# Modulation sums moved wholly to VectorE, with late fetches and a folding reduction

## The chip, the cores and the metric

One core of a Trainium2 chip runs the whole program. The metric is device time in microseconds from the first to the last instruction of one execution; a kernel's figure is the median of its runs.

## The reference

Two blocks run one after the other on 256 tokens of width 1024. Block 1 has two layers (three mixing branches, a gated feed-forward with 2816 hidden columns, a small gated embedding). Block 2 has two layers whose norms and residuals are modulated by vectors that depend on a conditioning vector `c` (for the latents) and `c_ctx` (for the context):

```python
s_lat = jax.nn.silu(c)
s_ctx = jax.nn.silu(c_ctx)[None, :]
for i in range(DEPTH):
    sh1, sc1, g1, sh2, sc2, g2 = jnp.split(s_lat @ ada_w[i] + ada_b[i], 6, axis=-1)
    a_l = modulate(rms_norm(h_lat, norm_g[i, 0]), sh1, sc1)
    if ctx_in:
        csh1, csc1, cg1, csh2, csc2, cg2 = jnp.split(s_ctx @ ada_w[i] + ada_b[i], 6, axis=-1)
```

`ada_w` is 2 x 1024 x 6144, 50 MB in fp32. The change concerns the product of these two vectors with `ada_w` alone. The product depends on nothing that block 1 computes, so it can be made during block 1.

## The kernel before

All weights come through one stream of 555 chunks of 128 x 1024 fp32 (512 KB each), in the order `ORDER`, into a ring of `RING` = 5 buffers `raw`. SP issues the fetch into a buffer when the chunk that is in it has been used up, strictly in order. A weight chunk ("split") is copied by ScalarE (ACT) into `whi` (line 1399, rounded to fp32r) and its remainder is put by GpSimd (POOL) into `wlo` (line 929, in four pieces for the chunks of each layer's first half, in one piece after that). ACT may write a `whi` buffer once TensorE (PE) has opened the chunk four ahead of it in the order; so PE, ACT and POOL walk along the stream together. A product of 128 x 256 takes per 128 rows of weights three matmuls (lines 980, 983, 984: high by high, high by low of the activations, low of the weights by high); a feed-forward tile `hg` or `hu` has 8 x 3 of them and uses one chunk, a down tile `dn` 11 x 3 and 1.375 chunks. Results go to four PSUM banks in rotation, counted by the semaphores `gemm_done` and `tiles_out`: PE may start tile n + 4 once VectorE (DVE) has moved tile n out. Each engine runs its own instruction list in order; the lists are written by loops over `TILES`.

A modulation chunk ("ada", later "mod") also sits in the stream and holds a `raw` buffer until it has been used. Before the change they are used in two ways:

- Block 2's layer 0 (the first 48 chunks): 12 tiles `("ada", n)` per layer of block 1, each two chunks and 8 fp32 matmuls with `silu_c` as stationary (function `modulation`, line 994; the trace shows each fp32 matmul as two). DVE adds each to `rows` (lines 1927, 1930). After four of them a tile `("turn", n)` turns the rows into columns (line 1002), and DVE adds the bias (line 1937). Four stand in the head of the layer (before `u` 1, `gl` 0, `("ss", "q")` and `rotk`), four among the third branch's gates, four in the feed-forward.
- Block 2's layer 1 (the last 48 chunks): in the first MLP of block 2, DVE multiplies each chunk's rows by the factor of their partition and adds them up in `mod_sums` in SBUF (`modulation_sum`, lines 1905 and 1907), and a tile `("sum", half)` for each of 12 half-parts adds the 128 partitions with matmuls of one column (line 1252): 16 of them, as the trace counts, for the 4 half-parts of both samples, 8 for the other 8.

The feed-forward of block 1 is evicted by DVE like this: a tile `hg` by one operation (line 2202); a tile `hu` by four (lines 2205, 2207, 2210, 1859), with ACT's tanh and copy between them; a tile `dn` by one (line 2199). In the head, ACT's square roots for the two small norms (line 1503) stand behind the `whi` copies that `keep_ahead` and `split_for` place there.

Of the kernel before, what the change touches and what calls it, by code (L numbers as in the profile page):

```python
# [61 lines left out]
for _name, _w in (("mix_g", 8), ("gate_b", 24), ("conv_w", 16), ("conv_b", 4), ("ba", 4), ("bx", 4), ("lam", 4),  # L62
# [8 lines left out]
            "wo": 8, "hg": 8, "hu": 8, "dn": 11, "pg": 8, "pp": 2, "ada": 0, "turn": 0}  # L71
# [10 lines left out]
ADA_TILES = DEPTH * 6 * D // 256  # L82
LAYER_ADA = 12
PLACES = 4


def with_modulation(tiles, places, first, flush=()):

    out, n, turned = [], first, first // PLACES
    for t in tiles:  # L90
        for _ in range(places.get(t, 0)):
            if n // PLACES > turned:
                out.append(("turn", turned))
# [25 lines left out]
MID_TILES, _n = with_modulation(MID_TILES, {("g", 2, 0): 1, ("g", 2, 2): 1, ("g", 2, 4): 1, ("g", 2, 6): 1}, _n,  # L119
                                flush=(("y", 2, 7),))  # L120
TAIL_TILES, _n = with_modulation(TAIL_TILES, {("hg", 0, 3): 1, ("hg", 0, 6): 1, ("hg", 0, 9): 1, ("dn", 0, 3): 1}, _n,
                                 flush=(("dn", 0, 6),))
assert _n == LAYER_ADA
FF_TILES = TAIL_TILES[TAIL_TILES.index(("hg", 0, 0)):TAIL_TILES.index(("dn", 1, 0))]
PLE_TILES = TAIL_TILES[TAIL_TILES.index(("pg", 0)):]
TILES = HEAD_TILES + MLA_FILL + FOX_FILL + MID_TILES + TAIL_TILES
# [32 lines left out]
ADA_CHUNKS = 2  # L159
assert PLACES * ADA_CHUNKS == KT  # L160


# [3 lines left out]
def chunk_plan(tiles, spans):  # L166

    order, at, adas, late, needed = [("split", n) for n in range(LEAD)], {}, 0, [], 0
    runs = {"ada": ADA_CHUNKS, "mod": 1}
    splits = LEAD  # L170
    for t in tiles:
        if t[1][0] in runs:
            run = [("ada", adas + i) for i in range(runs[t[1][0]])]
            adas += len(run)
# [12 lines left out]
def chunk_reach(tiles, spans, order, at):  # L187

    reach, needed, adas, read = {}, 0, 0, 0
    for t in tiles:  # L190
        first, to = spans.get(t, (0, 0))
# [4 lines left out]
        adas += {"ada": ADA_CHUNKS, "mod": 1}.get(t[1][0], 0)  # L196
        last = at[t] if needed == read else order.index(("split", needed - 1))
        r = min(last + AHEAD, len(order) - 1)
        while r + 1 < len(order):
            kind, n = order[r + 1]  # L200
            freed_by, m = order[r + 1 - RING] if r + 1 >= RING else ("split", 0)
            if kind == "split" and (n >= needed + SLOTS_AHEAD or (freed_by == "ada" and m >= adas)):
                break
            r += 1
        reach[t] = r
# [52 lines left out]
SUM_CHUNKS = 4  # L258
SUM_BEHIND = 2


def with_sums(tiles, places):

    out, n, due = [], 0, []
    for i, t in enumerate(tiles):
        if due and due[0][1] <= i:
            out.append(("sum", due.pop(0)[0]))
        for _ in range(places.get(t, 0)):
            out.append(("mod", n))
            n += 1  # L270
            if n % SUM_CHUNKS == 0:
                due.append((n // SUM_CHUNKS - 1, i + SUM_BEHIND))
        out.append(t)
    assert not due
    return out, n
# [2489 lines left out]
```

## Time and profile before

| what | value |
|---|---|
| median of 3 runs | 1834.68 us (1832.49 to 1835.5) |
| the profiled execution | 1833.74 us |
| its span | 1831.9 us |
| PE busy | 1738.3 us, 95% |
| POOL busy | 1172.0 us, 64% |
| ACT, DVE busy | 893.1 us and 891.2 us, 49% each |
| bytes read | 295.89 MB |

The profiled execution lies 0.94 us below the median, and 1.84 us above its span. Block 1's first layer runs from 0 to about 533 us, its second to about 1050 us, block 2 takes the rest. The feed-forward of the two layers lies at about 308 to 501 us and 824 to 1017 us.

### The profile page before, as it was taken

To read this page: it belongs to the slowest core of one execution; us is meant where nothing else is said; L and a number is where in the kernel's file an instruction comes from. 1 tells how busy PE (TensorE), PEld (TensorE's weight loads), DVE (VectorE), ACT (ScalarE), POOL (GpSimd) and SP (SyncE) were. 2 spreads that over 40 slices of the span, in tenths; PEclk is the share of its full clock that TensorE was granted. 3 is DMA by queue.
4 is the path that set the end of the run, shared out by engine and by line. 5 is a ranking of instruction groups with operands and counts; after the bars stand their busy time and mean duration, and the time that the engine had idled before them with its cause. 6 is when DMAs were issued, how large, how long until landed. Compare 5 with 4: busy or idle time off the path is not lost.

```text
span 1831.9 us, 32203 instructions
## 1 busy us (share of the span) xinstructions
PE 1738.3 (95%) x12690; PEld 1601.1 (87%) x12690; DVE 891.2 (49%) x2019; ACT 893.1 (49%) x1468; POOL 1172.0 (64%) x768
## 2 busy tenths in 40 slices
PE   6899999999999899999999969999999979889997
PEld 6788899999999788999999968888888778689997
DVE  6577445313365674353233666854444565642223
ACT  6545546444666455465445864232323353564443
POOL 6887678788878776677788623444444443058884
PEclk9999999999999899999999989999999999999999
DMA  6543465665555433666655503354453422035552
GB/s 238 192 144 127 133 236 190 226 212 184 176 188 185 154 128 129 235 200 214 219 185 175 199 26 127 140 194 163 171 183 139 172 93 81 24 116 186 182 184 81
DMA packets 83414, 299.02 MB, mean 163 GB/s; under 512 B 9152, under 2 KB 11456, under 8 KB 83008
## 3 DMA queue, kind: packets, MB, share of 16 engines
q1 hardware_dynamic: 81648, 294.02, 47.3%
q10 hardware_dynamic: 1616, 2.95, 0.5%
q8 instruction: 100, 1.64, 0.4%
q14 instruction: 50, 0.41, 0.1%
HBM read 295.89 MB, written 1.05 MB: 162 GB/s over the span
## 4 chain that ended last, share of the span: by engine, by line
PE 84%; DVE 7%; ACT 3%; issue 2%; POOL 2%; DVEq 1%; DMA 1%; ACTq 0%; SPq 0%
PE bank L980 25%; PE bank L984 24%; PE bank L983 24%; POOL wlo L929 2%; PE bank L994 1%; PE bank L1146 1%; PE bank L1160 1%; PE bank L1252 1%; PE bank L1176 1%; ACT whi L1399 1%; PE bank L1223 1%; DVE acts L2103 1%; PE bank L1226 1%; PE bank L1227 1%; PE bank L1149 1%
## 5 line engine op out<-in xcount | busy, mean ns | idle before, releaser
L929 POOL TENSOR_TENSOR wlo<-raw,whi 128x256 fp32r<-128x256 f32 (+1 forms) x756 | 1166.3, 1567 | 638.9 <-ACT whi L1399 638.3
L980 PE MATMUL bank<-split_acts,whi 128*128 128x256 f32 (+1 forms) x3492 | 1058.6, 303 | 26.7 <-DVE split_acts L1859 16.0
L983 PE MATMUL bank<-split_acts,whi 128*128 128x256 f32 (+1 forms) x3492 | 1046.1, 300 | 0.0
L984 PE MATMUL bank<-split_acts,wlo 128*128 128x256 f32 (+1 forms) x3492 | 1046.0, 300 | 0.0
L1399 ACT ACTIVATE whi<-raw 128x1024 fp32r<-128x1024 f32 x459 | 483.6, 1056 | 550.4 <-DMA raw<-in_stream 302.8
L980 PEld LDWEIGHTS bank<-split_acts,whi 128*128 128x128 f32 x3492 | 669.4, 192 | 68.3 <-issue 24.0
L983 PEld LDWEIGHTS bank<-split_acts,whi 128*128 128x128 f32 x3492 | 670.3, 192 | 20.6
L984 PEld LDWEIGHTS bank<-split_acts,wlo 128*128 128x128 f32 x3492 | 669.8, 192 | 21.0
L1859 DVE TENSOR_TENSOR split_acts<-bank,split_acts 128x256 fp32r<-128x256 f32 (+1 forms) x214 | 98.7, 461 | 50.2 <-ACT split_acts L1543 20.9
L2525 DVE SCALAR_TENSOR_TENSOR acts<-bank,acts 128x256 f32<-128x256 f32 x104 | 47.4, 481 | 149.5 <-PE bank L984 149.0
L1907 DVE SCALAR_TENSOR_TENSOR acts<-raw,acts 128x512 f32<-128x512 f32 x112 | 111.9, 1019 | 8.1 <-issue 2.5
L2539 DVE TENSOR_SCALAR acts<-bank 128x512 f32<-128x512 f32 (+1 forms) x64 | 35.6, 558 | 150.0 <-PE bank L984 141.5
L2205 DVE TENSOR_TENSOR bank<-bank,acts 128x256 f32<-128x256 f32 x44 | 19.0, 432 | 102.2 <-PE bank L984 102.2
L1726 ACT ACTIVATE bank<-acts 128x512 f32<-128x512 f32 (+1 forms) x64 | 31.3, 489 | 53.9 <-DVE acts L2539 53.9
L1509 ACT ACTIVATE acts<-acts 128x128 f32<-128x128 f32 (+1 forms) x64 | 28.6, 448 | 50.6 <-DVE acts L2112 50.6
L2196 DVE TENSOR_TENSOR acts<-bank,acts 128x256 f32<-128x256 f32 x32 | 13.6, 425 | 67.8 <-PE bank L984 67.8
L2166 DVE TENSOR_TENSOR acts<-bank,acts 128x256 f32<-128x256 f32 x48 | 20.4, 425 | 49.2 <-PE bank L984 47.3
L1445 ACT ACTIVATE bank<-acts 128x256 f32<-128x256 f32 x56 | 31.7, 566 | 19.6 <-DVE acts L2498 16.5
L1534 ACT ACTIVATE acts<-acts 128x256 f32<-128x256 f32 x48 | 24.2, 505 | 32.2 <-DVE acts L2166 32.2
L1543 ACT ACTIVATE split_acts<-bank 128x256 fp32r<-128x256 f32 x44 | 16.9, 384 | 46.0 <-DVE bank L2210 45.7
L2202 DVE TENSOR_TENSOR bank<-bank,acts 128x256 f32<-128x256 f32 x44 | 19.0, 433 | 36.0 <-PE bank L984 35.5
L1223 PE MATMUL bank<-split_acts,whi 128*128 128x256 f32 (+1 forms) x48 | 18.8, 393 | 18.5 <-DVE split_acts L1859 18.5
(277 smaller groups left out, 1610.5 us busy)
## 6 DMA issues: line engine op xcount, KB each, us to landing
raw<-in_stream SPq DMA_DIRECT2D x555, 512.0 KB, 3.6
acts<-in_x SPq DMA_DIRECT2D x1, 1024.0 KB, 6.1
acts<-in_ctx ACTq DMA_DIRECT2D x1, 1024.0 KB, 7.3
acts<-in_const ACTq DMA_DIRECT2D x1, 1024.0 KB, 5.2
out<-acts SPq DMA_DIRECT2D x8, 128.0 KB, 2.1
acts<-in_const SPq DMA_DIRECT2D x1, 711.0 KB, 8.2
acts<-in_p ACTq DMA_DIRECT2D x2, 256.0 KB, 3.9
acts<-in_const ACTq DMA_DIRECT2D x1, 320.0 KB, 3.0
```

The source lines that it names most:

```text
L929: last = nc.gpsimd.tensor_tensor(wlo[slot][:, cols], raw[source][:, cols], whi[slot][:, cols].bitcast(F32), ALU.subtract)
L980: first = nc.tensor.matmul(out_ap, w_hi, hi_act(k), start=(k == 0), stop=False)
L983: nc.tensor.matmul(out_ap, w_hi, lo_act(k), start=False, stop=False)
L984: last = nc.tensor.matmul(out_ap, w_lo, hi_act(k), start=False, stop=(k == k_tiles - 1))
L1223: one = nc.tensor.matmul(o, w_hi[:, cols], hi, start=(k == 0), stop=False)
L1399: sc.activation(whi[n % RING][:, :], raw[source % RING][:, :], ACT.Copy).then_inc(hi_ready, 1)
L1445: last = sc.activation(dst(t, s), side(tmp, t % 2, s), ACT.Identity, scale=gain_col(l, i, t, s), bias=mod_col(l, SH1 if i == 0 else SH2, t ...
L1726: sc.activation(hid_home[j % 3][:, a], tile(tmp, j % 2, 512)[:, a], ACT.Square)
L1859: return v.tensor_tensor(lo, value, hi.bitcast(F32), ALU.subtract)
L1907: last = v.scalar_tensor_tensor(out=total, in0=w, scalar=factor, in1=total, op0=ALU.mult, op1=ALU.add)
L2525: last = v.scalar_tensor_tensor(out=side(h, n, s), in0=src, scalar=col(s), in1=side(h, n, s), op0=ALU.mult, op1=ALU.add)
L2539: v.tensor_scalar(tile(tmp, j % 2, 512)[:, a], b[:, 0:w], 0.0, None, ALU.max)\
```

## The change

- All 96 modulation chunks are summed on DVE by `modulation_sum`. The 48 for block 2's layer 0 are used in block 1's feed-forward: 24 per layer, one ahead of the eviction of each of `hg` (0, 1 to 9), `dn` (0, 1 to 6) and `hg` (1, 0 to 8). Each has both samples, so four operations of 128 x 512 per chunk. The 48 others stay in block 2's first MLP, at places that shift by a few tiles.
- The partial sums lie in PSUM banks 6 and 7 in block 1, and in `v2` (SBUF) and bank 4 in block 2. `c_square` has two buffers instead of four for it.
- When the four chunks of a half are in, DVE reduces each sum of 128 x 512 to 128 x 16 with a `tensor_reduce` that transposes (line 1878). One tile `("sum",)` per stage (two in block 1, one in block 2) then adds what is left with four matmuls of 48 or 64 columns against a stack of four identities, `fold` (line 976).
- `fetch_tiles` puts a modulation chunk into the stream as if it were needed four tiles later than it is.
- The ada and turn tiles are gone, and `opening_gains` moves to behind `hu` (1, 9) of the second layer.

The core of the diff:

```diff
--- before.py
+++ after.py
@@
+SUM_CHUNKS = 4
+SUM_BEHIND = 2
+def with_sums(tiles, places):
+
+    out, n, last = [], 0, max(tiles.index(t) for t in places)
+    for i, t in enumerate(tiles):
+        if i == last + SUM_BEHIND:
+            out.append(("sum",))
+        for _ in range(places.get(t, 0)):
+            out.append(("mod", n))
+            n += 1
+        out.append(t)
+    return out, n
+FETCH_BEHIND = 4
+def fetch_tiles(tiles):
+
+    out, late, i = [], [], 0
     for t in tiles:
+        if t[0] == "mod":
+            late.append((t, i + FETCH_BEHIND))
+            continue
+        while late and late[0][1] <= i:
+            out.append(late.pop(0)[0])
         out.append(t)
+        i += 1
+    return out + [t for t, _ in late]
...
-HEAD_TILES, _n = with_modulation(HEAD_TILES, {("u", 1): 1, ("gl", 0): 1, ("ss", "q"): 1, ("rotk", 0): 1},
-                                 0, flush=(("kn", 2),))
...
+FFN_PLACES = {**{("hg", 0, j): 1 for j in range(1, 10)}, **{("dn", 0, n): 1 for n in range(1, 7)},
+              **{("hg", 1, j): 1 for j in range(9)}}
...
 MLP_PLACES = [((w, 0, q, j), 1) for q in range(QUARTERS)
-              for w, js in (("w1", range(2, 7) if q == 0 else range(1, 6)),
-                            ("w2", range(8 if q < 2 else 7 if q == 2 else 5))) for j in js]
+              for w, js in (("w1", range(5, 7) if q == 0 else range(1, 7)),
+                            ("w2", range(8 if q < QUARTERS - 1 else 4))) for j in js]
...
-        mod_sums = [[v2[:, (2 * i + s) * 512:(2 * i + s + 1) * 512] for s in range(2)] for i in range(2)]
+        folded = v2[:, 512:768]
...
-        c_square = [bank[4], bank[5], bank[6], bank[7]]
+        c_square = [bank[4], bank[5]]
+        mod_parts = [[bank[6][:, :], bank[7][:, :]]] * DEPTH + [[v2[:, 0:512], bank[4][:, :]]]
...
+            def sum_quadrants(b, stage):
+
+                pe.wait_ge(mod_summed, stage + 1)
+                n = len(SUM_SLOTS[stage])
+                parts = folded[:, 0:16 * n].rearrange("p (m q) -> p m q", q=4)
+                for q in range(4):
+                    nc.tensor.matmul(b[32 * q:32 * q + 32, 0:4 * n], C("fold"), parts[:, :, q], start=True, stop=True)
+                return pe.drain()
...
                 for k in (2 * pair, 2 * pair + 1):
                     v.drain()
                     for s in sides:
-                        w, total = raw[c % RING][:, k % 2 * 512:(k % 2 + 1) * 512], mod_sums[half % 2][s]
+                        w = raw[c % RING][:, k % 2 * 512:(k % 2 + 1) * 512]
                         factor = silu_c[:, 2 * k + s:2 * k + s + 1]
                         if k == 0:
-                            last = v.tensor_scalar(total, w, factor, None, ALU.mult)
+                            last = v.tensor_scalar(parts[s], w, factor, None, ALU.mult)
                         else:
-                            last = v.scalar_tensor_tensor(out=total, in0=w, scalar=factor, in1=total, op0=ALU.mult,
-                                                          op1=ALU.add)
+                            last = v.scalar_tensor_tensor(out=parts[s], in0=w, scalar=factor, in1=parts[s],
+                                                          op0=ALU.mult, op1=ALU.add)
                 last.then_inc(mod_used, 1)
                 if pair == SUM_CHUNKS - 1:
-                    v.drain().then_inc(mod_summed, 1)
...
+                    v.drain()
+                    for s in sides:
+                        i = SUM_SLOTS[stage].index((half, s))
+                        last = v.tensor_reduce(folded[:, 16 * i:16 * i + 16],
+                                               parts[s].rearrange("p (b j) -> p b j", j=32), axis=AXX, op=ALU.add,
+                                               apply_transpose=True)
+                    if half == STAGE_SUMS[stage][-1]:
+                        last.then_inc(mod_summed, 1)
```

The rows that follow are the instruction lists, in order of the program, without times. On PE, in the third branch of layer 0 of block 1, around the tile `("ada", 4)`; before:

```order
L983 MATMUL bank<-split_acts,whi 128x256
L984 MATMUL bank<-split_acts,wlo 128x256
L994 MATMUL bank<-raw,acts 32x256 x8
L980 MATMUL bank<-split_acts,whi 128x256
L983 MATMUL bank<-split_acts,whi 128x256
```

The eight matmuls read the raw chunk; this row is gone at all 24 places. On PE in the feed-forward of layer 0, between `hu` (1, 8) and `hg` (1, 9); now:

```order
L966 MATMUL bank<-split_acts,whi 128x256
L967 MATMUL bank<-split_acts,wlo 128x256
L976 MATMUL bank<-acts 32x48 x4
L963 MATMUL bank<-split_acts,whi 128x256
L966 MATMUL bank<-split_acts,whi 128x256
```

The row with L976 is new; before, the products of the two tiles followed each other directly.

On DVE in the same feed-forward, from the last step of `hu` (0, 0) through `hu` (0, 1) to the chunk ahead of `hg` (0, 2); now (L2164 evicts `hg`, L2167 to L1822 evict `hu`):

```order
L1822 TENSOR_TENSOR split_acts<-bank,split_acts 128x256
L1869 TENSOR_SCALAR bank<-raw,acts 128x512 x2
L1871 SCALAR_TENSOR_TENSOR bank<-raw,acts,bank 128x512 x2
L2164 TENSOR_TENSOR bank<-bank,acts 128x256
L2167 TENSOR_TENSOR bank<-bank,acts 128x256
L2169 SCALAR_TENSOR_TENSOR acts<-acts,bank 128x256
L2172 SCALAR_TENSOR_TENSOR bank<-acts,bank 128x256
L1822 TENSOR_TENSOR split_acts<-bank,split_acts 128x256
L1871 SCALAR_TENSOR_TENSOR bank<-raw,acts,bank 128x512 x4
L2164 TENSOR_TENSOR bank<-bank,acts 128x256
```

The rows L1869 and L1871 are new; each stands ahead of an eviction that PE waits for in the end.

On ACT in the head of a layer of block 1, from the wide square root of the first branch (L1592, now L1555) to the two small ones (L1503, now L1466); before:

```order
L1592 ACTIVATE acts<-acts 128x1024
L1399 ACTIVATE whi<-raw 128x1024 x2
L1503 ACTIVATE acts<-acts 128x256 x2
L1399 ACTIVATE whi<-raw 128x1024 x6
```

and now:

```order
L1555 ACTIVATE acts<-acts 128x1024
L1362 ACTIVATE whi<-raw 128x1024 x4
L1466 ACTIVATE acts<-acts 128x256 x2
L1362 ACTIVATE whi<-raw 128x1024 x4
```

Two more chunks are copied ahead of the small roots, and there are no modulation chunks between the chunks any more.

## Rows read from the trace of the kernel before

**Rows 1.** The page: busy us (share of the span) and instructions of each engine.

```profile
PE 1738.3 (95%) x12690; PEld 1601.1 (87%) x12690; DVE 891.2 (49%) x2019; ACT 893.1 (49%) x1468; POOL 1172.0 (64%) x768
```

**Rows 2.** Busy time by stretch: us, PE, PEld, DVE, ACT, POOL, PE clock, DMA share, GB/s.

```profile
414.00:506.00 92.00, 92.00 (x767) 91.95 (x766) 32.40 (x77) 52.08 (x78) 74.94 (x32) 1.00 0.56 181
```

**Rows 3.** Timeline of PE around an ada tile of the feed-forward: start, duration.

```profile
384.00 0.28 PE L984 MATMUL bank<-split_acts,wlo 128*128 128x256 f32 x1
384.20 1.07 PE L994 MATMUL bank<-raw,acts 128*32 128x256 f32 x16
385.41 0.38 PE L980 MATMUL bank<-split_acts,whi 128*128 128x256 f32 x1
```

**Rows 4.** Timeline of PE around a turn tile (397) and a sum tile (1138).

```profile
397.26 0.28 PE L984 MATMUL bank<-split_acts,wlo 128*128 128x256 f32 x1
...
397.74 0.36 PE L980 MATMUL bank<-split_acts,whi 128*128 128x256 f32 x1
...
1138.40 0.39 PE L983 MATMUL bank<-split_acts,whi 128*128 128x512 f32 x1
1138.63 0.39 PE L984 MATMUL bank<-split_acts,wlo 128*128 128x512 f32 x1
...
1140.56 0.49 PE L980 MATMUL bank<-split_acts,whi 128*128 128x512 f32 x1
```

**Rows 5.** Timelines of POOL and PE in the heads of layers 0 and 1.

```profile
23.82 38.63 POOL L929 TENSOR_TENSOR wlo<-raw,whi 128x256 fp32r<-128x256 f32 x48 [5.86 <-ACT whi L1399]
...
47.24 0.35 PE L980 MATMUL bank<-split_acts,whi 128*128 128x256 f32 x1 [1.07 <-POOL wlo L929]
...
543.91 24.11 POOL L929 TENSOR_TENSOR wlo<-raw,whi 128x256 fp32r<-128x256 f32 x28 [0.35 <-ACT whi L1399]
...
569.02 0.28 PE L980 MATMUL bank<-split_acts,whi 128*128 128x256 f32 x1
```

**Rows 6.** DVE's timeline, then the chain that ended last, in layer 0's head.

```profile
81.05 1.41 DVE L2303 TENSOR_SCALAR acts<-bank,acts 128x512 f32<-128x512 f32 x2
...
78.18 0.96 ACT whi L1399
...
82.06 3.28 DMA raw<-in_stream
85.42 1.06 ACT whi L1399
...
89.57 1.76 DVE acts L2103
...
91.47 0.98 PE bank L1066 x4
```

**Rows 7.** Timelines of DVE (`hu` evicted), ACT and POOL (one chunk) in the feed-forward.

```profile
411.69 0.43 DVE L2205 TENSOR_TENSOR bank<-bank,acts 128x256 f32<-128x256 f32 x1 [2.45 <-PE bank L984]
...
413.42 0.43 DVE L1859 TENSOR_TENSOR split_acts<-bank,split_acts 128x256 fp32r<-128x256 f32 x1 [0.45 <-ACT split_acts L1543]
...
371.84 1.06 ACT L1399 ACTIVATE whi<-raw 128x1024 fp32r<-128x1024 f32 x1 [1.43 <-PE bank L980]
...
372.97 2.41 POOL L929 TENSOR_TENSOR wlo<-raw,whi 128x1024 fp32r<-128x1024 f32 x1 [0.48 <-ACT whi L1399]
```

**Rows 8.** DVE: one modulation chunk; then single lines, ns min/median/max or mean.

```profile
1118.67 2.90 DVE L1907 SCALAR_TENSOR_TENSOR acts<-raw,acts 128x512 f32<-128x512 f32 x4
...
L1907 DVE SCALAR_TENSOR_TENSOR acts<-raw,acts 128x512 f32<-128x512 f32 x112 | 111.9, 1019 | 8.1 <-issue 2.5
...
L2210 DVE SCALAR_TENSOR_TENSOR bank<-acts,bank x44: 428/429/430, 312.1 to 986.0; 128x256 f32<-128x256 f32 x44
...
L2472 DVE TENSOR_TENSOR acts<-bank,acts 128x512 f32<-128x512 f32 x6 | 4.2, 692 | 0.5
...
L2676 DVE RECIPROCAL acts<-acts 128x512 f32<-128x512 f32 x4 | 13.4, 3352 | 0.3
```

**Rows 9.** The page: DMA issues, KB each, median us from issue to landing.

```profile
raw<-in_stream SPq DMA_DIRECT2D x555, 512.0 KB, 3.6
```

More of the change, by code:

```diff
@@ L135, in modulation_before @@
     for t in tiles:
-        if t[0] in ("ada", "turn", "mod", "sum"):
+        if t[0] in ("mod", "sum"):
             run.append(t)
@@ L158 @@
 ATOM_SPAN, LAYER_ATOMS = first_atoms()
-ADA_CHUNKS = 2
-assert PLACES * ADA_CHUNKS == KT
 LEAD = 2
 def chunk_plan(tiles, spans):
-    order, at, adas, late, needed = [("split", n) for n in range(LEAD)], {}, 0, [], 0
-    runs = {"ada": ADA_CHUNKS, "mod": 1}
+    order, at, mods, late, needed = [("split", n) for n in range(LEAD)], {}, 0, [], 0
     splits = LEAD
     for t in tiles:
-        if t[1][0] in runs:
-            run = [("ada", adas + i) for i in range(runs[t[1][0]])]
-            adas += len(run)
+        if t[1][0] == "mod":
+            run = [("mod", mods)]
+            mods += 1
             if splits > needed:
@@ L255 @@
     + [("ss", 1, 1)] + mlp_tiles(1) + [("ss", "last")])
[L258 to L275, printed above, removed]
 MLP_PLACES = [((w, 0, q, j), 1) for q in range(QUARTERS)
-              for w, js in (("w1", range(2, 7) if q == 0 else range(1, 6)),
-                            ("w2", range(8 if q < 2 else 7 if q == 2 else 5))) for j in js]
+              for w, js in (("w1", range(5, 7) if q == 0 else range(1, 7)),
+                            ("w2", range(8 if q < QUARTERS - 1 else 4))) for j in js]
 ALL_TILES2, _n = with_sums(TILES2, dict(MLP_PLACES))
-MODS = _n
-assert 2 * DEPTH * LAYER_ADA + MODS == DEPTH * 6 * KT
+assert DEPTH * LAYER_MODS + _n == DEPTH * 6 * KT
 BEFORE2 = modulation_before(ALL_TILES2)
@@ L412, in shape_constants @@
     put(c, CONST, "sub", np.stack([(i // 32) % 2 == 0, (i // 32) % 2 == 1], 1))
-    put(c, CONST, "strips", np.stack([i == 32 * s + sample for s in range(4) for sample in range(2)], 1))
+    put(c, CONST, "fold", np.tile(np.eye(32), (4, 1)))
     d = np.zeros((P, NCONST2), np.float32)
@@ L481, in layer_atoms @@
     for t in TILES:
-        if t in SHARED or t[0] in ("ada", "turn"):
+        if t in SHARED or t[0] == "sum":
             continue
@@ L952, in _ @@
                 atom = 0
-                ada = 0
             def weights(n):
@@ L1040, in gemm @@
                     b = open_bank(t)
[L1041 to L1047 removed]
+                    if kind == "sum":
+                        sum_quadrants(b, lay).then_inc(gemm_done, 1)
                         return
@@ L1248, in gemm2 @@
                 elif kind == "sum":
-                    pe.wait_ge(mod_summed, t[1] + 1)
-                    for s in sum_of(t[1])[2]:
-                        for i in range(4):
-                            last = nc.tensor.matmul(b[:, 2 * i + s:2 * i + s + 1], tile(mod_sums[t[1] % 2][s], i, P),
-                                                    ones[:, 0:1], start=True, stop=True)
+                    last = sum_quadrants(b, SECOND)
                 elif kind == "py":
@@ L2379, in _ @@
                 for t in MID_TILES:
-                    if t[0] not in ("ada", "turn"):
-                        of_tile(t)
+                    of_tile(t)
                 merged_lo(7)
```

178 lines of the change are left out of this document (64 added, 114 removed).

## The prediction

> **What bounds the kernel now.** I read the page first, then the busy time by stretch, then the timelines around each thing that the change removes. TensorE (PE) is busy 95% of the span; VectorE (DVE) and ScalarE (ACT) are at 49% [rows 1]. In the feed-forward of block 1 PE has no idle time: 92.00 us busy of 92.00 with 767 matmuls, which is 0.12 us each, while POOL is busy 74.94 us and DVE 32.40 [rows 2]. So a matmul taken out there shortens the kernel, and DVE has room until its work per tile exceeds PE's. The exceptions are in the heads of block 1's layers, where PE waits for POOL or for the small norms.
>
> **What is removed from PE.** Around an ada tile the last product before starts at 384.00 and the next one after at 385.41: 1.41 us where 0.12 is the usual step, so 1.29 us each [rows 3]. A turn costs 397.74 - 397.26 - 0.12 = 0.36 us. A sum with 16 matmuls costs 1140.56 - 1138.63 = 1.93 us where the step is 0.23, so 1.70 us, or 0.106 per matmul [rows 4]; the 12 sums have 4 x 16 + 8 x 8 = 128 matmuls, 13.6 us, in an MLP where PE is as gapless as in the feed-forward. This term I take whole.
>
> Of the 24 ada tiles 16 stand in the middle and the feed-forward of the two layers, in gapless PE work: 16 x 1.29 = 20.6 us. All 6 turns: 2.2 us. The 8 in the heads are another matter:
> - Layer 0, before `u` 1 and `gl` 0. POOL works without a pause from 23.82 for 48 pieces (12 chunks in 38.63 us, 3.2 us a chunk, where a tile of 24 matmuls takes 2.88), and at 47.24 PE waits 1.07 us for it [rows 5]. POOL's run begins after ACT's root of the first norm, ahead of both ada tiles in effect. PE gets to the same wait earlier and leaves it at the same time: 0 us.
> - Layer 1, the same two. POOL's run of 28 pieces from 543.91 ends at 568.02, and PE opens that chunk at 569.02 [rows 5]. Only the 1.0 us between them is to be had of 2.6.
> - Both layers, before `("ss", "q")` and `rotk`. PE waits here for two roots and two reciprocals until 91.47. The chain comes through the fetch into the buffer that POOL had just freed (3.28 us), and the copy to `whi` at 85.42 that stands ahead of ACT's roots [rows 6]. Without modulation chunks in the ring the chunks behind are there already. ACT then copies four chunks in a row, as it copied one at 78.18 (ending at 79.14 [rows 6]): it is free at 79.1 + 3 x 1.05 = 82.3. DVE has moved the `fv` tiles out at 82.5 (81.05 + 1.41 [rows 6]). With 0.43 for the variance the roots can start at 82.95. From their start (85.42 + 1.06) to PE at 91.47 it took 5.0 us; so PE goes on at 88.0, 3.4 us earlier. I take the same for layer 1: 6.8.
>
> Heads together: 0 + 1.0 + 6.8 = 7.8 us. Gross gain: 20.6 + 2.2 + 13.6 + 7.8 = 44.2 us.
>
> **What is added to PE.** Three sum tiles of four small fp32 matmuls with a drain. The trace has no such tile; the ada tile with 16 traced matmuls costs 1.29 [rows 3], the turn with four and no drain 0.36 [rows 4]. These are the two bounds. It has four (eight traced) and the drain; I take 0.8, 2.4 us in all (1.1 to 3.9).
>
> **What is added to DVE.** 96 operations of 128 x 512 per feed-forward, four per chunk. In block 2 four such take 2.90 us without disturbance [rows 8]. That is 725 ns each; the mean there is 1019 [rows 8], which I put down to waits for POOL, as both inputs come from SBUF. In the new form one input and the output lie in PSUM. The nearest row of that form, L2210 (SBUF and PSUM in, PSUM out, 256 columns), runs at 428 to 430 ns over 44 instances although POOL is busy 75 of 92 us there [rows 2, 8]. So contention shouldn't touch it, and 512 columns with a bank operand take 692 ns (L2472), not more than 725. I take 2.9 us a chunk with its drain, 2.7 to 4.1 as bounds. The first of a half, a `tensor_scalar` from SBUF into PSUM, I price alike.
>
> The transposing `tensor_reduce` of 512 columns isn't in the trace. Bounds: 0.69 for one pass over 512 columns, as L2472 [rows 8], 3.35 for the slowest operation on 512 (the reciprocal) [rows 8]. I take 0.7: it is one pass, so 1.4 us per half. The Trainium skill ("VectorE: DVE Perf Modes", section "Rules for kernel authors") expects `tensor_reduce` at the 1x rate and calls it the slowest DVE op on a hot path; at the 1x rate it stays near 0.7 us, so this speaks for the lower bound; no run of this kernel shows it yet.
>
> Does DVE keep up? A pair `hg` and `hu` is 48 matmuls, 5.76 us. DVE needs 0.5 for `hg`, 2.16 for `hu` (411.69 to 413.85) [rows 7], and 2.9 for the chunk: 5.5 us, plus 1.4 each fourth time. It is full, with some 1.5 us of lag after nine pairs. `hg` (0, 10) and `dn` (0, 0), without a chunk, clear this. PE may run ahead of the eviction by four banks, and lag below some 4.8 us costs nothing: `hu` j is out 2.1 us after its end now, its `hg` 1.2 earlier, and the `hg` bank is wanted 5.76 after the end of `hu`.
>
> In the `dn` part the fetch comes late. Count from the first product of `dn` (0, 0) as 0; a chunk opens each 2.88 us, a `dn` tile ends each 3.96. ACT starts a copy when PE opens the chunk four ahead; POOL ends 3.5 us later (371.84 to 375.38) [rows 7]; the landing takes 3.4 to 3.6 more [rows 9]. Modulation chunk 9 goes into the buffer of weight chunk 102, whose partner 98 opened at -0.9; POOL is done at 3.0, landing 6.5. DVE would have wanted it at 4.4. It is used up at 9.4, chunk 10 (buffer of 104) lands at 12.5 and is done at 15.4, chunk 11 lands at 18 and is done at 21, with the reduction at 22.5; `dn` (0, 3), which PE ended at 15.84, is out at 23.0 and its bank is wanted at 27.7. The lag goes down from there. In layer 1 `ctx_sum` adds 0.5 us per `dn` tile. By this count no bank is late, the tightest by 1.7 us.
>
> The lag comes due at the sum, which PE wants at the end of `hu` (1, 8). In layer 0 `hu` (1, 1) is out 8.8 us after its pair began; six pairs at -0.26 and one reduction later it is 8.7, so DVE starts the last chunk 2.9 us into the pair of `hg` (1, 8) and is done with it and the reductions at 2.9 + 2.9 + 1.6 = 7.4, where PE wants them at 5.76: a stall of 1.7 us. In layer 1 the same count gives 9.5, a stall of 3.8. Together 5.5 us. In block 2 the last chunk is two tiles of 5.2 us ahead of the sum, no stall; of DVE's 128 operations there 96 get their sum in PSUM and may run faster, but nothing waits for them.
>
> DMA: two weight chunks and one modulation chunk in 5.76 us are 1.57 MB, 273 GB/s, against 181 GB/s at a share of 0.56 [rows 2], 323 at full share. It fits, with less room; I price it at 0.
>
> **Sum.** 44.2 - 2.4 - 5.5 = 36.3 us. The profiled execution takes 1833.7, so 1797; the median of the runs lies 0.94 higher, and so my number is 1834.7 - 36.3 = 1798 us.
>
> **Rivals.**
> - A: PSUM operands are dearer, and the lag grows. For it: the first input from SBUF still pays there, and no 512-column instance of the form exists. Against: L2210's 429 ns. Priced with 0.3 us more per chunk: 15 chunks from the `dn` part to the sum are 4.5 us per layer, so 1798 + 9 = 1807. The Trainium skill ("VectorE: DVE Perf Modes", section "The TRN2 errata") gives a PSUM source 62 cycles more than an SBUF one, which works out to an estimate of 0.26 us per chunk; the rows here show the opposite order, 692 against 725 ns.
> - B: DVE becomes the bound (the other side). If the new form waits for POOL as L1907 does, at 1019 ns, a chunk takes 1.3 us more. Layer by layer: 9 x 1.3 less 4.8 of slack is 7 us, 15 x 1.3 is 20 more, 27 a layer: 1798 + 54 = 1852. It decides from x more per chunk where 2 x (24x - 4.8) = 36.3, x = 0.96, that is 0.92 us an operation. A reduce at 3.35 us would come to much the same (5.3 us more at each of six halves). Against it stands L2210.
> - C: late fetches. If landings take 5 us or more at 273 GB/s, each `dn` tile with a chunk slips by 1.5 us, SP's strict order holds weight chunks back, and the 1.7 us of room is gone: 5 to 8 us a layer, 1811.
> - D: more is gained than I count, since the sums find DVE free and POOL's runs in the heads shorten with DVE's two-SBUF work moved: up to 5.5 + 4 us, 1789.
>
> **How the numbers follow.** Forecast (1792 to 1804) 0.55, A 0.13, B 0.07, C 0.12, D 0.13. The range for 8 in 10 takes the forecast with most of A, C and D: 1788 to 1812. Slower by over 0.2% (about what a measurement can tell here) only in B past its deciding point: 0.06; within 0.2%: 0.03; faster: 0.91.
>
> **What would show it.** Right: no L994 and L1002, PE without gaps at the feed-forward's tiles, a wait of PE at each of the two sums of 1 to 4 us; the new SCALAR_TENSOR_TENSOR near 0.69 us with a maximum close to its minimum; the wait at `("col", "kv")` ending near 88 us; POOL's first run and PE's wait at 47 us unchanged. Wrong: PE waiting for DVE at `hg` or `dn` (A or B by the duration), SP or DVE waiting for landings (C), a `tensor_reduce` of microseconds.

## The result, and the profile after

| what | before | after |
|---|---|---|
| median of the runs | 1835.09 us (1832.49 to 1836.05, 4 runs) | 1809.65 us (1806.54 to 1813.14, 4 runs) |
| ratio | | 0.9869, 95% interval 0.985 to 0.9887 |
| the profiled execution, its span | 1833.74 us, 1831.9 us | 1806.54 us, 1804.7 us |

The changed kernel is 25.4 us faster by the medians and 27.2 us by the profiled spans. Forecast were 36.3 us and 1798; the result lies inside the range of 1788 to 1812, 12 us above the number.

Line numbers shift with the change: the products are now lines 963, 966 and 967, the small products of a sum tile 976, the modulation operations 1869 and 1871, the reduction 1878, `hg` 2164, `hu` 2167, 2169, 2172 and 1822, `dn` 2161, POOL's piece 913. The page first, its busy line and its row of the fetches, which answer to [rows 1] and [rows 9]:

```profile
PE 1700.6 (94%) x12178; PEld 1578.1 (87%) x12178; DVE 1024.2 (57%) x2211; ACT 891.2 (49%) x1468; POOL 1163.8 (64%) x768
...
raw<-in_stream SPq DMA_DIRECT2D x555, 512.0 KB, 3.4
```

PE has 37.7 us less work but the span is only 27.2 shorter, so PE now stands idle or slow somewhere. The busy time by stretch (columns as in [rows 2]) says where. The first row is the stretch of [rows 2] in layer 0's feed-forward, which now comes 17 us sooner; the other two are parts of it.

```profile
397.00:489.00 92.00, 86.58 (x715) 86.23 (x714) 56.22 (x112) 46.08 (x73) 71.63 (x30) 0.96 0.66 222
...
414.00:440.00 26.00, 26.00 (x219) 26.00 (x219) 21.68 (x41) 11.27 (x18) 19.88 (x9) 1.00 0.77 259
440.00:450.00 10.00, 4.58 (x32) 4.23 (x31) 7.44 (x16) 3.76 (x6) 6.65 (x3) 0.66 0.76 265
```

PE has no gap for 26 us, and then in 10 us does 4.58 us of work at a clock of 0.66. PE's timeline there (start, duration, and in brackets the idle time before and what ended it):

```profile
440.59 0.28 PE L967 MATMUL bank<-split_acts,wlo 128*128 128x256 f32 x1
...
446.18 0.39 PE L976 MATMUL bank<-acts 128*32 128x48 f32 x8 [5.32 <-DVE acts L1878]
446.67 0.58 PE L963 MATMUL bank<-split_acts,whi 128*128 128x256 f32 x1
...
449.40 0.41 PE L963 MATMUL bank<-split_acts,whi 128*128 128x256 f32 x1
449.61 0.35 PE L966 MATMUL bank<-split_acts,whi 128*128 128x256 f32 x1
449.79 0.28 PE L967 MATMUL bank<-split_acts,wlo 128*128 128x256 f32 x1
```

It is the sum tile. PE waits 5.32 us for DVE's reduction. After it, products start 0.21 us apart instead of 0.12 until 449.6, since the granted clock has fallen. The windows put both such stretches, one in each layer, at 0.50, the lower of the clock's two levels (1.2 GHz):

```profile
442.90:449.70 6.80, 3.42 (x22) 3.27 (x23) 5.19 (x12) 1.72 (x3) 4.25 (x3) 0.50 0.80 293
951.50:958.30 6.80, 3.52 (x22) 3.36 (x23) 5.09 (x12) 1.72 (x3) 4.24 (x3) 0.50 0.79 275
```

About half of that stretch lies under the wait. What PE still works of it, 14 products from 446.67 to 449.6, costs 14 x 0.09 = 1.3 us. The waits of PE over the whole program (total, times, longest) name what is new, the first and third of these rows; the middle one is the wait in both heads:

```profile
PE bank L976 <- DVE acts L1878: 11.0, 2, 5.7
...
PE bank L1033 <- DVE acts L2065: 9.9, 2, 4.9
...
PE bank L963 <- DVE acts L2169: 2.4, 3, 1.2
```

Why DVE is late at the sum is in its own timeline. It answers to [rows 7, 8]:

```profile
435.92 2.90 DVE L1871 SCALAR_TENSOR_TENSOR bank<-raw,acts,bank 128x512 f32<-128x512 f32 x4
438.92 0.43 DVE L2164 TENSOR_TENSOR bank<-bank,acts 128x256 f32<-128x256 f32 x1
...
440.32 0.43 DVE L2172 SCALAR_TENSOR_TENSOR bank<-acts,bank 128x256 f32<-128x256 f32 x1
...
441.73 2.90 DVE L1871 SCALAR_TENSOR_TENSOR bank<-raw,acts,bank 128x512 f32<-128x512 f32 x4
444.72 1.32 DVE L1878 TRANSPOSE_TENSOR_REDUCE acts<-bank 128x16 f32<-128x512 f32 x2
446.13 0.43 DVE L2164 TENSOR_TENSOR bank<-bank,acts 128x256 f32<-128x256 f32 x1
```

None of these rows has idle time before it; in the whole cycle the profile marks one wait of DVE, 0.45 us inside `hu` for ACT's copy, as before the change [rows 7]. From one chunk to the next DVE takes 441.73 - 435.92 = 5.81 us, PE's pair 5.76. A reduction adds 1.4 us (446.13 - 444.72). So once DVE is behind, it stays behind and falls further back with each reduction.

The modulation operations themselves, ns min/median/max; the second row is block 2's form with its sums in SBUF, the third the reduction:

```profile
L1871 DVE SCALAR_TENSOR_TENSOR bank<-raw,acts,bank x252: 741/754/758, 304.1 to 1408.8; 128x512 f32<-128x512 f32 x126
L1871 DVE SCALAR_TENSOR_TENSOR acts<-raw,acts x28: 750/752/2769, 1115.1 to 1207.8; 128x512 f32<-128x512 f32 x28
...
L1878 DVE TRANSPOSE_TENSOR_REDUCE acts<-bank x36: 672/717/718, 323.0 to 1409.6; 128x16 f32<-128x512 f32 x36
```

Last the heads, PE's timeline at the two places of [rows 5, 6]:

```profile
46.72 0.36 PE L963 MATMUL bank<-split_acts,whi 128*128 128x256 f32 x1 [0.94 <-POOL wlo L913]
...
87.41 0.98 PE L1033 MATMUL bank<-acts 1*128 1x1 f32 x4 [4.94 <-DVE acts L2065]
```

The wait for POOL ends 0.5 us sooner than before (47.24), the wait for the norms 4.1 us sooner (91.47).

**Where the time went.** The order of the weight chunks is the same in both kernels. So the two traces can be laid beside each other by the moment at which PE opens each chunk; nearly every step of the difference stands at one edit. The steps sum to the 27.2 us; the last row is what the others leave.

| step | forecast | measured |
|---|---|---|
| 16 ada tiles in gapless work | 20.6 | 22.2 (16 x 1.39) |
| 6 turns | 2.2 | 2.6 (6 x 0.43) |
| 12 sums of block 2 | 13.6 | 15.0 (4 x 1.85 + 8 x 0.95) |
| head of layer 0, of layer 1 | 3.4, 4.4 | 4.4, 6.4 |
| layer 0: sum tile, stall and clock | -2.5 | -7.4 |
| layer 1: the same, and waits for banks | -4.6 | -11.1 |
| end of layer 1, block 2: its sum tile and the rest | -0.8 | -4.9 |
| in all | 36.3 | 27.2 |

### The profile page after: what moved, and what is told of

The parts are those of the page before. It is cut to its first block, busy times and chain, and to the rows that moved or that the text cites. A ratio compares the mean times of both kernels' runs of the same rounds, so it can differ in the third digit from the quotient of the medians.

```text
span 1804.7 us, 31385 instructions
## 1 busy us (share of the span) xinstructions
PE 1700.6 (94%) x12178; PEld 1578.1 (87%) x12178; DVE 1024.2 (57%) x2211; ACT 891.2 (49%) x1468; POOL 1163.8 (64%) x768
## 4 chain that ended last, share of the span: by engine, by line
PE 68%; DVE 13%; POOL 5%; DVEq 4%; ACT 4%; issue 3%; DMA 2%; ACTq 0%; SPq 0%
PE bank L963 20%; PE bank L967 19%; PE bank L966 19%; POOL wlo L913 5%; DVE bank L1871 3%; DVEq L1864 2%; DMA raw<-in_stream 1%; DVEq L2016 1%; DVE split_acts L1822 1%; PE bank L1113 1%; DVE bank L2164 1%; PE bank L1127 1%; DVE bank L2172 1%; PE bank L1143 1%; DVE acts L2169 1%
## 5 line engine op out<-in xcount | busy, mean ns | idle before, releaser
L1871 DVE SCALAR_TENSOR_TENSOR bank<-raw,acts,bank 128x512 f32<-128x512 f32 x252 | 182.0, 752 | 30.0 <-DMA raw<-in_stream 17.8
L1822 DVE TENSOR_TENSOR split_acts<-bank,split_acts 128x256 fp32r<-128x256 f32 (+1 forms) x214 | 98.7, 461 | 49.7 <-ACT split_acts L1506 19.9
L1502 ACT ACTIVATE acts<-bank 128x256 f32<-128x256 f32 x44 | 16.9, 385 | 129.0 <-DVE bank L2164 128.5
L2158 DVE TENSOR_TENSOR acts<-bank,acts 128x256 f32<-128x256 f32 x32 | 13.6, 425 | 67.5 <-PE bank L967 67.5
L1871 DVE SCALAR_TENSOR_TENSOR acts<-raw,acts 128x512 f32<-128x512 f32 x28 | 31.9, 1141 | 2.4 <-issue 0.2
L1690 ACT ACTIVATE split_acts<-acts 128x512 fp32r<-128x512 f32 (+1 forms) x64 | 32.6, 509 | 0.0
```

The source lines that it names most:

```text
L1690: sc.activation(tile(hid_hi, j, 512)[:, a], tile(tmp, j % 2, 512)[:, a], ACT.Square)\
L1822: return v.tensor_tensor(lo, value, hi.bitcast(F32), ALU.subtract)
L1871: last = v.scalar_tensor_tensor(out=parts[s], in0=w, scalar=factor, in1=parts[s], op0=ALU.mult, op1=ALU.add)
```

## The experiments

Each but e5 changes the changed kernel. The kernel before ran on the same chip in each of the three groups, 1833.75, 1834.92 and 1834.85 us in this order. Theory 1 throughout: DVE's work per pair is no less than PE's, so its lag is kept up to the sum tile and is paid there.

| run | median us | ratio to before, interval |
|---|---|---|
| e1_sum_later | 1801.06 | 0.9828 (0.9809 to 0.9847) |
| e2_fetch_behind_2 | 1811.74 | 0.9886 (0.9867 to 0.9906) |
| e3_sums_in_sbuf | 1952.27 | 1.0651 (1.0634 to 1.0667) |
| e4_no_ops | 1791.46 | 0.9772 (0.9755 to 0.9788) |
| e5_changed_again | 1811.34 | 0.9864 (0.9847 to 0.9881) |
| e6_spread | 1822.08 | 0.993 (0.9918 to 0.9942) |
| e7_spread_later | 1808.94 | 0.9866 (0.9845 to 0.9887) |
| e8_spread_later_fetch_2 | 1805.53 | 0.9842 (0.9826 to 0.9858) |
| e9_two_to_dn | 1807.92 | 0.9847 (0.9829 to 0.9865) |
| e10_one_to_hg_0_10 | 1804.0 | 0.9841 (0.9823 to 0.9859) |
| e11_two_to_dn_fetch_2 | 1805.79 | 0.985 (0.9833 to 0.9866) |
| e12_sum_later_again | 1797.94 | 0.9794 (0.9779 to 0.9809) |

### What PE waits for at the sum (e1, e2, e3, e4)

**e1**: the sum tile of a layer stands in front of `hu` (1, 10) instead of `hg` (1, 9).

```diff
-def with_sums(tiles, places):
+def with_sums(tiles, places, behind=SUM_BEHIND):
...
-        if i == last + SUM_BEHIND:
+        if i == last + behind:
...
-ALL_TAIL_TILES, LAYER_MODS = with_sums(TAIL_TILES, FFN_PLACES)
+ALL_TAIL_TILES, LAYER_MODS = with_sums(TAIL_TILES, FFN_PLACES, behind=5)
...
-                        if (part, j) == (1, 9) and lay == DEPTH - 1:
+                        if (part, j) == (1, 10) and lay == DEPTH - 1:
```

> The changed kernel, but the sum tile of each layer of block 1 stands five tiles behind the last modulation chunk's tile (before hu (1,10)) instead of two. Theory 1, the sum stands where VectorE is not done: TensorE's waits of 5.3 and 5.7 us and the half clock behind each (1.3 us) go, so 13 us less than the changed kernel, about 1797. Theory 2, VectorE's lag is what costs and the wait only moves: TensorE waits as long at dn (1,0) for the last hidden tile, the time stays within 3 us of 1807 to 1810.

The wait for L1878 is gone. Beside the changed kernel, PE loses 7.4 us (layer 0) and 7.8 us (layer 1) less at the sum tile's former place. Of this 3.4 us in layer 0 and 5.1 in layer 1 are given back, 0.65 each for the sum tile in its new place and the rest in short waits for banks, some of them ahead of the sum: the lag is still there and now shows at the next thing that PE wants from DVE. So 1801.06 us lies between the two theories: the wait at the sum goes, as theory 1 says, and a part of it moves, as theory 2 says.

**e2**: the fetches two tiles behind their place instead of four (`FETCH_BEHIND = 2`).

> The changed kernel, but modulation chunks stand two tiles behind their place in the stream instead of four. If late landings in the dn part (VectorE waits 9 us for them per layer) are where the lag at the sum comes from, these waits go, TensorE's wait at the sum falls to under 2 us and its bank waits in layer 1 (2.4 us) vanish: about 1798. If the lag comes from VectorE's work per pair (5.81 us against 5.76), VectorE's waits go but the wait at the sum stays above 4 us: 1806 or more. If raw buffers are held too long, TensorE or ACT waits for weights: above 1810.

DVE's waits for landings fall from 17.8 to 5.1 us (the first row, from DVE's waits), while PE's wait at the sums stays (the second, from PE's):

```profile
DVE bank L1871 <- DMA raw<-in_stream: 5.1, 3, 2.7
```

```profile
PE bank L976 <- DVE acts L1878: 11.4, 2, 5.7
```

So lateness of the fetches isn't the cause of the stall, and the time is no lower. It is no higher either: 1811.74 us is above the 1810 that stood for the third case, but the changed kernel itself took 1811.34 in e5, and in the feed-forwards PE waits for no weights.

**e3**: the partial sums of block 1 in SBUF, in a part of `v2`, instead of PSUM.

```diff
-        mod_parts = [[bank[6][:, :], bank[7][:, :]]] * DEPTH + [[v2[:, 0:512], bank[4][:, :]]]
+        mod_parts = [[v2[:, 1024:1536], v2[:, 1536:2048]]] * DEPTH + [[v2[:, 0:512], bank[4][:, :]]]
```

> The changed kernel, but the partial sums of block 1 lie in SBUF instead of PSUM banks 6 and 7. If the PSUM operand is what keeps VectorE free of waits for POOL, the operations go from 752 ns to 1.2 us or more on average, VectorE becomes the bound of the feed-forward (24 chunks x 1.8 us or more per layer) and the time passes that of the kernel before: 1850 to 1900. If contention isn't decided by that, the operations stay near 0.75 and the time within 3 us of the changed kernel.

The time passes the expected 1850 to 1900 by 52 us. The operation is the same, its operands lie elsewhere. DVE's line 1871 by form (ns min/median/max), one chunk in DVE's timeline with POOL's beside it, and PE's waits:

```profile
L1871 DVE SCALAR_TENSOR_TENSOR acts<-raw,acts x196: 737/752/2910, 310.3 to 1354.9; 128x512 f32<-128x512 f32 x196
L1871 DVE SCALAR_TENSOR_TENSOR bank<-raw,acts,bank x84: 741/755/758, 1262.8 to 1555.9; 128x512 f32<-128x512 f32 x84
```

```profile
333.03 6.32 DVE L1871 SCALAR_TENSOR_TENSOR acts<-raw,acts 128x512 f32<-128x512 f32 x4
```

```profile
332.10 5.21 POOL L913 TENSOR_TENSOR wlo<-raw,whi 128x1024 fp32r<-128x1024 f32 x2 [4.00 <-ACT whi L1362]
```

```profile
PE bank L963 <- DVE acts L2169: 66.5, 28, 4.6
PE bank L976 <- DVE acts L1878: 23.3, 2, 12.4
PE bank L963 <- DVE acts L2161: 22.9, 10, 4.4
```

The median is the same, 752 against 754 ns, but single ones take up to 2910, and the mean over the 168 in block 1 is 1457. That is the mechanism of rival B, and with its own formula, at 4 x (1.457 - 0.725) = 2.9 us more per chunk, it gives 1798 + 2 x (24 x 2.9 - 4.8) = 1928 us; 1952 were measured. In the changed kernel it doesn't occur, since no PSUM instance exceeds 758 ns. The traces also say what the slow ones wait for. Of the 168, 69 take 1300 ns or more, and POOL is at work during at least 70% of each of them; the other 99 take at most 754 ns, and 92 of these have no work of POOL beside them. With the sums in PSUM 151 of block 1's 168 lie wholly beside POOL's work and none takes over 758. This is read from the traces; no run without POOL's work was made.

**e4**: block 1's modulation operations behind the first 128-row block of each half are left out, with one `memset` per chunk in their place; chunks are fetched and released as before, and block 2's layer 0 gets a modulation that lacks them.

```diff
                 for k in (2 * pair, 2 * pair + 1):
+                    if stage < SECOND and k and k % 2 == 0:
+                        continue
                     v.drain()
+                    if stage < SECOND and k:
+                        last = v.memset(stat[:, 15:16], 0.0)
+                        continue
```

> The changed kernel without VectorE's modulation operations in block 1, except those of the first row tile of each half (one memset per chunk instead); the modulation of block 2's first layer comes out wrong. All fetches, buffers, sum tiles stay. It gives the gain without VectorE's load: if all of TensorE's loss in the feed-forward is VectorE's load, the two waits at the sums go and the time is about 1792 to 1795; if a part is contention for memory or fetches that hold back the weights, it stays above 1800.

1791.46 us. PE's waits at the sums and layer 1's waits for banks are gone; beside the changed kernel 6.7 and 7.2 us come back at the sums and 1.3, 0.4 and 1.4 us at layer 1's banks; what stays is 0.65 us at each sum tile. The stretches of above in this kernel: 13.23 us of DVE's work in 26 us instead of 21.68, and a clock of 1.00 behind it.

```profile
414.00:440.00 26.00, 26.00 (x219) 26.00 (x218) 13.23 (x34) 12.97 (x19) 21.62 (x10) 1.00 0.77 264
440.00:450.00 10.00, 9.89 (x88) 9.56 (x88) 4.21 (x12) 4.80 (x7) 7.43 (x5) 1.00 0.74 263
```

With the same traffic in the queues (share 0.77) PE loses nothing. So the loss in the feed-forward is DVE's load and not the transfers.

### Is it the number of chunks in the second half? (e5 to e8)

**e5** is the changed kernel again, as the yardstick of this group.

> The changed kernel, unaltered, as the yardstick of this group: 1806 to 1813 us, ratio 0.985 to 0.989. PE waits about 5.3 and 5.7 us for the reduction at the two sum tiles and 2.4 us in layer 1 for banks.

1811.34 us, the waits about as before (11.4 at the sums, now 5.7 at each, and 2.7 at the banks, now in both layers).

**e6**: three chunks of each layer leave the second half of the feed-forward.

```diff
-FFN_PLACES = {**{("hg", 0, j): 1 for j in range(1, 10)}, **{("dn", 0, n): 1 for n in range(1, 7)},
-              **{("hg", 1, j): 1 for j in range(9)}}
+FFN_PLACES = {**{("hg", 0, j): 1 for j in range(1, 11)}, **{("dn", 0, n): 1 for n in range(8)},
+              **{("hg", 1, j): 1 for j in range(6)}}
```

> Three of each layer's 24 fetches and chunks move out of the second half of the feed-forward (hg(1,6) to hg(1,8)) into hg(0,10), dn(0,0) and dn(0,7); the sum tile still stands two tiles behind the last chunk, so now at hg(1,6). Theory 1 (what PE waits for at the sum is the last chunk and its reduction, late by VectorE's queue, and that queue does not shrink in pairs that hold a chunk): 5 to 7 us of wait at each sum as before, but no bank waits after it: 1804 to 1810. Rival (the queue is piled up mainly by the nine pairs of the second half, so six leave less): 2 to 3 us of wait at each sum, 1799 to 1803.

1822.08 us: both theories missed it, by 12 us and more. The wait at the sums is the same (11.7 in two), as theory 1 had it, but PE has a new one inside `dn` (0, 0), before the last three of its 33 products. PE's timeline, then DVE's:

```profile
361.48 0.28 PE L967 MATMUL bank<-split_acts,wlo 128*128 128x256 f32 x1
364.18 0.39 PE L963 MATMUL bank<-split_acts,whi 128*128 128x256 f32 x1 [2.42 <-DVE split_acts L1822]
```

```profile
358.42 2.90 DVE L1871 SCALAR_TENSOR_TENSOR bank<-raw,acts,bank 128x512 f32<-128x512 f32 x4
...
363.70 0.42 DVE L1822 TENSOR_TENSOR split_acts<-bank,split_acts 128x256 fp32r<-128x256 f32 x1 [0.45 <-ACT split_acts L1506]
```

The last 128 rows of `dn` (0, 0) need what DVE makes of `hu` (0, 10). The chunk that now stands in front of `hg` (0, 10) holds this up by its 2.9 us, and PE works its tiles in order. With the clock at half behind the wait it costs 4.2 us in layer 0 and 6.6 in layer 1 (from where PE opens the chunks). Waits for banks ahead of the sums, 1.8 us in layer 0 and 2.8 in layer 1, come on top.

**e7** has the same places and the sum tile four tiles behind the last chunk (`behind=4`); **e8** also the fetches at 2.

> The same moved chunks, and the sum tile four tiles behind the last chunk instead of two (at hg(1,7)). Theory 1: four pairs without a chunk follow the last one, each takes VectorE 2.8 us against PE's 5.8, so neither the sum nor a bank is waited for: 2 x 7.4 us and some of the 3.1 us of layer 1's bank waits come back, 1791 to 1796. Rival (the queue only shifts to bank waits, as behind a late sum without moved chunks): 1798 to 1802.

> As the run before, with the fetches two tiles behind their places instead of four. Theory 1 (landings do not bind): the same time within 2 us, 1790 to 1797. Rival (late landings hold what is left of the loss): 2 to 4 us less than the run before.

e7: 1808.94 us, e8: 1805.53. The waits for the reduction at the sums are gone in both, as expected, but theory 1 had no wait at all there, and 2.8 and 1.2 us of waits for banks stand at the sum tiles instead. The loss inside `dn` (0, 0) remains, which wasn't known when this was written, and so both are slower than expected. The two agree within their intervals, so the landings don't decide here either.

### Which of the moved chunks costs (e9 to e12)

All four have a late sum tile. **e9** moves two chunks of each layer to `dn` (0, 0) and `dn` (0, 7); **e10** moves only one, to `hg` (0, 10); **e11** is e9 with fetches at 2; **e12** is e1 again. The lines that are added:

```diff
 # e9, e11
+FFN_PLACES = {**{("hg", 0, j): 1 for j in range(1, 10)}, **{("dn", 0, n): 1 for n in range(0, 8)},
+              **{("hg", 1, j): 1 for j in range(7)}}
 # e10
+FFN_PLACES = {**{("hg", 0, j): 1 for j in range(1, 11)}, **{("dn", 0, n): 1 for n in range(1, 7)},
+              **{("hg", 1, j): 1 for j in range(8)}}
 # all three
+ALL_TAIL_TILES, LAYER_MODS = with_sums(TAIL_TILES, FFN_PLACES, behind=4)
```

> Sum tile at hg(1,8), last chunk at hg(1,6); two chunks of each layer moved to dn(0,0) and dn(0,7), none to hg(0,10). Theory (the loss of the two runs with spread chunks came from the chunk in front of hg(0,10), which keeps VectorE from the last low part that PE needs for dn(0,0)): no wait for L1822 at dn(0,0), no wait at the sum, under 2 us of bank waits: 1796 to 1801, at or a little under the kernel whose sum alone is later. Rival (chunks at the edges of the dn part are what cost): 1803 to 1809 with waits at dn(0,0) or hg(1,0).

> Only one chunk of each layer moved, from hg(1,8) to hg(0,10); sum tile at hg(1,9). Theory (a chunk in the last pair before the handover is paid in full): PE waits 2 to 3 us for L1822 at dn(0,0), and runs at half clock behind it, 4 to 5 us a layer in all, less 1 to 2 us of bank waits that the shorter second half saves: 1804 to 1810. Rival (edges of the dn part): 1799 to 1802.

> As the run with two chunks moved to dn(0,0) and dn(0,7), with fetches two tiles behind their places. Theory (VectorE's work binds, not the landings): within 2 us of that run, 1795 to 1801. Rival (chunks in the dn part come late from memory and their lateness reaches the second half): 2 to 4 us less.

> The changed kernel with the sum tile at hu(1,10) alone, again, beside these three: 1799 to 1804 us, ratio 0.981 to 0.985.

e10, 1804.0 us, has the wait for L1822 inside `dn` (0, 0), 2.48 us in layer 0 and 3.97 in layer 1, and loses 4.2 and 5.5 us there against e12. So it is the chunk in the last pair before the handover that costs, as the theory said. A further 4.1 us are lost at layer 1's sum tile, by two short waits like those that e9 shows next.

e9, 1807.92 us, doesn't have that loss, as the theory said, but its time lies in the rival's range, for two other reasons. PE's timeline at its sum tile, and the window behind it:

```profile
439.62 0.28 PE L967 MATMUL bank<-split_acts,wlo 128*128 128x256 f32 x1
441.11 0.36 PE L976 MATMUL bank<-acts 128*32 128x48 f32 x8 [1.21 <-DVE acts L2169]
442.52 0.58 PE L963 MATMUL bank<-split_acts,whi 128*128 128x256 f32 x1 [1.04 <-DVE split_acts L1822]
```

```profile
442.90:445.60 2.70, 2.70 (x14) 2.70 (x14) 1.87 (x7) 1.77 (x4) 2.70 (x2) 0.50 0.29 74
```

The sum tile takes a bank of the four in its turn, waits for it, and the next product waits again. Behind these two short waits the clock is at 0.50 for a dozen products: 4.3 us in all, the sum tile's own 0.65 included, and as much in layer 1. The half clock isn't certain, though. In e7, behind waits of 1.45 and 1.04 us at the same two places, it stays at 1.00, and the loss is 3.1 us:

```profile
437.80:440.50 2.70, 2.64 (x22) 2.64 (x23) 1.95 (x6) 2.27 (x5) 2.70 (x2) 1.00 0.16 61
```

The other reason is at the edge of the `dn` part, where the rival had it: in layer 1 PE waits 2.1 us in front of `hg` (1, 1) for the eviction of a `dn` tile (3.8 us lost). In e11 this wait is gone, but one of 1.8 us for a bank stands two tiles behind it, with half clock too (3.5 us lost), and more is lost at layer 1's sum; over layer 1's feed-forward e11 loses 11.2 us and e9 12.4. The earlier fetches gain little, and the two end within their error, both above what was expected. In e12 the tile stands where DVE has had a pair without a chunk. PE waits once, for a bank, and not at the sum tile; the clock stays at 1.00 from 444 to 460 us:

```profile
448.56 0.39 PE L963 MATMUL bank<-split_acts,whi 128*128 128x256 f32 x1 [1.21 <-DVE acts L2169]
...
451.42 0.28 PE L967 MATMUL bank<-split_acts,wlo 128*128 128x256 f32 x1
451.63 0.36 PE L976 MATMUL bank<-acts 128*32 128x48 f32 x8
452.10 0.38 PE L963 MATMUL bank<-split_acts,whi 128*128 128x256 f32 x1
```

e12 comes to 1797.94 us, a little under its expectation, and with e1 is the best version here, e4 aside: 37 and 33 us under the kernel before on the same chip, and 12 and 9 us under the changed kernel's 1809.65. The program is the same in both, and yet e12's profiled span is 7.3 us under e1's (its profiled execution, 1792.92 us, lies 5 us under its own median): 3.0 us of it in layer 1's head, 3.1 in layer 1's first `dn` part, where e1 waits 2.1 us for banks and e12 doesn't. So single steps of 1 to 3 us differ from run to run, which is why the comparisons above go by place.

## Why the prediction was right, and where it was off

That 1809.65 us lies inside the range is in part luck. By the table the gains came out 6.4 us larger than counted (50.6 against 44.2) and the losses 15.5 us larger (23.4 against 7.9); only their difference of 9.1 us shows in the profiled executions.

- **PE's removed work** (36.4 us forecast, 39.8 measured): right in kind, small in size. The first product behind an ada tile takes 0.38 us instead of 0.28 [rows 3] and holds up the next one too; I counted to its start, 1.29 us, and 1.39 came back, each time to the hundredth. The turns and the sums of block 2 have the same tenth.
- **Heads** (7.8 forecast, 10.8 measured): the split held. Nothing came from layer 0's first two tiles: the 0.5 us that are there stand already at the first product. From layer 1's came 0.4, where 2.8 us were gained and 2.3 given back to POOL. PE went on behind the norms at 87.4 us in layer 0, where 88.0 was worked out. Layer 1's chain gave 6.0 us where I copied layer 0's 3.4. Of these 1.5 us stand at 621.8 to 625.2 us, where the kernel before has a half-clock stretch and the changed kernel's trace has none. In e5, the same program as the changed kernel, there is one, and the 1.5 us are missing; so they belong to the execution and not to the change. For the other 1.1 us no run gives a reason.
- **The failed step: "six pairs at -0.26 and one reduction later it is 8.7".** A pair with a chunk was put at 5.5 us, its terms 0.5, 2.16 and 2.9 being 5.56, and takes 5.81: 3.00 for the chunk with the gap behind it, 2.81 for `hg` and `hu` (441.73 - 438.92), where I added durations and left out the 0.1 us between instructions and 0.2 us inside `hu` (2.36 against 2.16). So the lag doesn't shrink at all. From the start of its pair to the end of its eviction `hu` (1, 1) to (1, 8) take 10.4, 10.4, 10.5, 11.9, 12.0, 12.4, 12.4 and 13.9 us in layer 0; in e4, without the operations, each takes 8.1 or 8.2. Six times 0.31 is 1.9 us, and another 1.6 us stood already at `hu` (1, 1): it was out 10.4 us after its pair began, not 8.8 (12.0 in e5, so this part differs between executions). In layer 1 it was out after 14.1 us, and PE's waits for banks then hold the value between 12.9 and 14.4. DVE was done with the reduction 11.1 us after the pair of `hg` (1, 8) began instead of 7.4. Stalls of 5.3 and 5.7 us stand where 1.7 and 3.8 were forecast. e4 shows that DVE's work is the whole of it, e2 that the landings are not.
- **Two costs had no term.** Half clock behind each stall, 1.3 us; and layer 1's waits for banks, 2.4 us, 3.1 with their effects. I had written that no bank is late, the tightest by 1.7 us; with the larger lag this room was gone in layer 1.
- **The sum tile's own cost** was 0.8 us in block 1 (5.3 and 1.3 of the 7.4 us are wait and clock; 0.65 in e4, where nothing is waited for) and 0.75 in block 2, about as taken.
- **Block 2 and the end of layer 1**: 4.1 us more than the sum tile were lost behind 958 us. The visible part of it is where half-clock stretches fall. In the kernel before one lies at 1471.7 to 1478.5; in the changed kernel they lie at 1436.2 to 1439.6, 1443.0 to 1449.8 and 1480.6 to 1487.4, and the steps of -1.6 and -2.4 us stand at these places. In e5 the stretch at 1436 and the step of -1.6 us are both missing, so this one belongs to the execution; the step of -2.4 is in e5 too. Why the stretches fall where they do no run tested.
- **DVE's prices** held: 754 ns against 725, the reduction 0.72 against 0.7, maximum next to minimum. The Trainium skill ("VectorE: DVE Perf Modes", section "Rules for kernel authors") has `tensor_reduce` at the 1x rate; the 717 ns for 512 columns agree, next to the 692 of a plain pass [rows 8]. By that page of the Trainium skill, section "The TRN2 errata", a PSUM source is dearer; the medians of e3 and of the changed kernel, 752 in SBUF and 754 in PSUM, show no such difference in this operation, nor do the changed kernel's reductions, 717 from PSUM and 712 from SBUF.
- **The rivals.** A: its time, 1807, is near the result and its second half, the lag grows, is what happened, but its cause is not: the operand isn't dearer, the count of gaps was short. B is real where the sums lie in SBUF (e3) and absent in PSUM. Its price was a little off in itself: 4 x (1.019 - 0.725) is 1.2 us a chunk and not 1.3, and x = 0.96 is 0.965 us an operation and not 0.92. C: DVE does wait 17.8 us for landings in all, and PE stays without a gap through the `dn` part, so it cost nothing in the changed kernel. D: the heads gave 3.0 us more, PE's work 3.4, and the sums the contrary. Of the signs of being wrong, waits of PE for DVE's evictions (three, up to 1.2 us) and waits of DVE for landings (nine, up to 5.5 us) were both there.

## What to carry to other kernels

When work is moved to an engine that keeps pace with the bottleneck, sum its cycle by the start-to-start distances in the trace and not by the durations: here 5.81 instead of 5.5 against 5.76 decided between a lag that drains and one that stays. An engine at 100% of the pace is fine as long as nobody asks it for its last result; put the consumer (here the sum tile, three tiles later for 9 to 12 us) where the engine has had a pair without the extra work, and keep that work out of the last step before every other handover (`hg` (0, 10): 4.2 and 5.5 us in e10 for one chunk of 2.9). Count the consumer's turn in the rotation of banks too.

## What the runs showed of the hardware

- Same operation, same size, one operand moved: with its running sum in SBUF a SCALAR_TENSOR_TENSOR of 128 x 512 had a median of 752 ns and a mean of 1457 (up to 2910) in block 1, slow only beside POOL's work (e3); with the sum in PSUM all 252 lay between 741 and 758, beside POOL's work or not.
- In block 1's feed-forwards the granted clock was at 0.50 for a time after every wait of PE of 1.98 us or more (2.48 us in e10, 2.09 in e9, 1.98 to 10.9 in e3), and stayed at 1.00 after every one of 1.70 us or less that stood alone. In between 1.77 us lowered it in e11, and 1.82 didn't in e3. After 1.21 and 1.04 us with only a sum tile's products between them it was at 0.50 in e9; after 1.45 and 1.04 us it was at 1.00 in e7. So a stall here cost up to twice its length (4.2 us for 2.48 in e10, 3.5 for 1.77 in e11).
- A transposing reduction of 128 x 512 takes 672 to 718 ns, about as much as a plain pass (692).
